# A transformer kernel on one core: the squares of a residual are summed on VectorE before TensorE takes them, and a stage's first two product blocks are interleaved by row

## The reference

```python
def rms_norm(x, gain):
    xf = x.astype(jnp.float32)
    y = xf * lax.rsqrt(jnp.mean(xf * xf, axis=-1, keepdims=True) + EPS)
    return (y * gain.astype(jnp.float32)).astype(x.dtype)
...
h = h + mix                                    # residual, r = 1, 5, 10, 14
h = h + conv_ffn(rms_norm(h, ffn_norm[layer]), ...)   # residual, r = 4, 8, 13, 17
```

## Time and profile before

| | |
|---|---|
| runs, us | 2889.69, 2891.96, 2896.49 |
| profiled execution, its own time | 2890.2 us |
| its span | 2888.4 us |
| mean granted TensorE clock | 0.985 of 2.4 GHz |
| busy: TensorE, VectorE, ScalarE, GpSimd | 96%, 60%, 36%, 3% |

### The profile page before, as it was taken

The page is one execution under the profiler, slowest core; times in us unless marked ns, Lnnn a source line. Parts: engine busy times, 40 slices in busy tenths (PEclk is TensorE's granted clock), DMA queues, the critical chain, the costliest instruction groups (busy, mean ns, idle before and its releaser), DMA issues.

```text
span 2888.4 us, 35842 instructions
## 1 busy us (share of the span) xinstructions
PE 2773.1 (96%) x14656; PEld 2250.6 (78%) x14656; DVE 1728.3 (60%) x2488; ACT 1028.3 (36%) x1495; POOL 90.1 (3%) x156
## 2 busy tenths in 40 slices
PE   7999799999998999999999999999999999999998
PEld 6778688888875588888776688888888787888886
DVE  4287657475668557575556647564665888553443
ACT  3244434242333534242434633232332222432322
POOL 0000000000001300000001400000000000000000
PEclk9999999999999999999999999999999999999999
DMA  6711024443232124343321025454432110333221
GB/s 162 158 44 44 30 89 149 126 143 108 73 97 81 30 85 153 124 141 111 88 82 44 1 65 193 159 178 138 143 100 70 34 33 26 107 104 100 88 92 41
DMA packets 261803, 276.85 MB, mean 96 GB/s; under 512 B 23496, under 2 KB 230856, under 8 KB 261641
## 3 DMA queue, kind: packets, MB, share of 16 engines
q1 hardware_dynamic: 231448, 219.51, 25.0%
q10 hardware_dynamic: 30192, 55.05, 5.9%
HBM read 267.19 MB, written 7.34 MB: 95 GB/s over the span
## 4 chain that ended last, share of the span: by engine, by line
PE 86%; DVE 7%; ACT 2%; DMA 2%; issue 1%; SPq 1%; ACTq 0%; POOL 0%; DVEq 0%
PE ps L554 23%; PE ps L556 23%; PE ps L555 23%; PE ps L1154 3%; PE ps L790 2%; PE ps L1186 2%; PE ps L918 1%; DMA sb<-in_hgrn_w_in 1%; PE ps L1113 1%; PE ps L935 1%; PE ps L612 1%; DVE sb L1826 1%; PE ps L1132 1%; DVE sb L2192 1%; PE ps L952 1%
## 5 line engine op out<-in xcount | busy, mean ns | idle before, releaser
L554 PE MATMUL ps<-sb 128*128 128x512 f32 (+2 forms) x3448 | 1286.7, 373 | 31.6 <-ACT sb L1388 5.5
L556 PE MATMUL ps<-sb 128*128 128x512 f32 (+2 forms) x3448 | 1268.0, 368 | 0.0
L555 PE MATMUL ps<-sb 128*128 128x512 f32 (+2 forms) x3448 | 1267.9, 368 | 0.0
L554 PEld LDWEIGHTS ps<-sb 128*128 128x128 f32 x3448 | 651.2, 189 | 162.0 <-issue 36.0
L556 PEld LDWEIGHTS ps<-sb 128*128 128x128 f32 x3448 | 650.7, 189 | 112.4
L555 PEld LDWEIGHTS ps<-sb 128*128 128x128 f32 x3448 | 651.3, 189 | 108.9 <-issue 1.2
L1826 DVE TENSOR_TENSOR sb<-sb 128x2048 fp32r<-128x2048 f32 (+2 forms) x196 | 438.4, 2237 | 357.8 <-ACT sb L1287 357.8
L1287 ACT ACTIVATE sb<-sb 128x2048 fp32r<-128x2048 f32 (+2 forms) x196 | 365.0, 1862 | 286.1 <-PE ps L556 266.7
L2062 DVE SCALAR_TENSOR_TENSOR sb<-ps,sb 128x511 f32<-128x511 f32 (+1 forms) x264 | 197.5, 748 | 172.2 <-ACT sb L1511 166.7
L1511 ACT ACTIVATE sb<-ps,sb 128x512 f32<-128x512 f32 x132 | 99.7, 772 | 233.7 <-PE ps L556 233.6
L2082 DVE SCALAR_TENSOR_TENSOR sb<-sb 128x512 f32<-128x512 f32 x168 | 126.0, 750 | 12.9 <-DVE sb L2082 0.5
(11 more groups left out here) (226 smaller groups left out, 2170.8 us busy)
## 6 DMA issues: line engine op xcount, KB each, us to landing
sb<-in_ffn_w_up SPq DMA_DIRECT2D x88, 1024.0 KB, 5.1
sb<-in_ada_w ACTq DMA_DIRECT2D x192, 256.0 KB, 3.2
sb<-in_ffn_w_down SPq DMA_DIRECT2D x32, 1024.0 KB, 5.0
sb<-in_ffn_w_down SPq DMA_DIRECT2D x16, 768.0 KB, 4.4
sb<-in_hy_w_in SPq DMA_DIRECT2D x12, 1024.0 KB, 5.1
sb<-in_hgrn_w_in SPq DMA_DIRECT2D x8, 1024.0 KB, 11.5
sb<-in_hgrn_w_in SPq DMA_DIRECT2D x16, 512.0 KB, 5.5
sb<-in_dsa_w_in SPq DMA_DIRECT2D x6, 1024.0 KB, 5.2
```

Source lines behind the costliest of these rows:

```text
L554: pe.matmul(o, al, bh, start=f, stop=False, **kw)
L555: pe.matmul(o, ah, bl, start=False, stop=False, **kw)
L556: m = pe.matmul(o, ah, bh, start=False, stop=l, **kw)
```

## The change

Two things change. First, VectorE adds up the squares of tiles 0 to 5: the square of tile 0 is written to `total` (`sq[1]`), the squares of tiles 1 to 6 to `one` (`sq[0]`), and `accumulate` adds `one` to `total` after tiles 1 to 5. TensorE sums `total` once, after the last block's first part, then tiles 6 and 7. The addition for tile j-1 stands on VectorE behind the addition of x tile j; the one for tile 5 behind `ahead(keys[2])`. The square of tile j waits for the addition of tile j-1, the square of tile 7 for TensorE's sum of `total`. At r = 8 both sets are treated so. Second, `halved_start` takes both blocks together for the first half: per row 12 matmuls, for 4 banks, which are waited for at the start; the second half's last sums stand after row 2, its spreading after row 5.

```diff
--- before.py
+++ after.py
@@ -650,8 +650,7 @@
                     project_half(key, j, 0, b, range(kt), ready, tile).then_inc(*mark(sem, ("res", r, 6 + j, 0)))
                     freed[b] = [("x", r, 6 + j, 0)]
                     if j == 0:
-                        squared(4)
-                        squared(5)
+                        squared(None)
                 for j in range(2):
                     b, part = banks[0][j], (kt - 2, kt // 2)[j]
                     wait_bank(b)
@@ -667,30 +666,35 @@
             def halved_start(sem, r, keys, banks, done, then):
 
                 stage, i = NEXT[r]
-                for half in range(2):
-                    ready = lambda k: [("h", stage, half, k, "hi"), ("h", stage, half, k, "lo")]
+                ready = lambda half, k: [("h", stage, half, k, "hi"), ("h", stage, half, k, "lo")]
+                for n in range(2):
+                    for b in banks[n]:
+                        wait_bank(b)
+                for k in range(NT):
                     for n in range(2):
-                        if half == 0:
-                            for b in banks[n]:
-                                wait_bank(b)
-                        for k in range(NT):
-                            for j in range(2):
-                                m = project_half(keys[n], j, half, banks[n][j], (k,), ready)
-                                if half and k == NT - 1:
-                                    m.then_inc(*mark(sem, done[n][j], *([("used", keys[n])] if j else [])))
-                                    freed[banks[n][j]] = then[n][j]
-                            if half == 0 and n == 0 and k == 2:
-                                squared_half(r, 1)
-                        if half == 0 and n == 0:
-                            spread_half(stage, i, 1)
-
+                        for j in range(2):
+                            project_half(keys[n], j, 0, banks[n][j], (k,), lambda k: ready(0, k))
+                    if k == 2:
+                        squared_half(r, 1)
+                    elif k == 5:
+                        spread_half(stage, i, 1)
+                for n in range(2):
+                    for k in range(NT):
+                        for j in range(2):
+                            m = project_half(keys[n], j, 1, banks[n][j], (k,), lambda k: ready(1, k))
+                            if k == NT - 1:
+                                m.then_inc(*mark(sem, done[n][j], *([("used", keys[n])] if j else [])))
+                                freed[banks[n][j]] = then[n][j]
             def residual(sem, r, keys, banks, ready, tile=None, stats=True, gain=False, amid=None, late=None):
                 def squared(j):
+
                     for i in ((0, 1) if gain else (0,)):
-                        if j == 0:
+                        if j is None:
                             wait_bank((STAT, OTHER)[i])
-                        pe.wait_ge(*at("sq", r, i, j))
-                        sums((STAT, OTHER)[i], (ht if i else sq)[j % 2], j == 0, j == NT - 1).then_inc(
+                            pe.wait_ge(*at("acc", r, i, 5))
+                        else:
+                            pe.wait_ge(*at("sq", r, i, j))
+                        sums((STAT, OTHER)[i], (ht if i else sq)[1 if j in (None, 7) else 0], j is None, j == NT - 1).then_inc(
                             *mark("pe_stat", ("sq_used", r, i, j), *([("stat", r, i)] if j == NT - 1 else [])))
 
                 for n in range(4):
@@ -706,14 +710,10 @@
                         halved_end(sem, r, keys[n], banks, ready, tile, squared)
                     elif stats and n == 3:
                         project(sem, keys[n], banks[n % 2], names, then, tile=tile, ready=ready, cols=(0,))
-                        squared(4)
-                        squared(5)
+                        squared(None)
                         project(sem, keys[n], banks[n % 2], names, then, tile=tile, ready=ready, cols=(1,))
                     else:
                         project(sem, keys[n], banks[n % 2], names, then, tile=tile, ready=ready)
-                        if stats and n:
-                            squared(2 * n - 2)
-                            squared(2 * n - 1)
                 if stats and r not in NEXT:
                     squared(6)
                     squared(7)
@@ -1337,7 +1337,7 @@
             def squares_half(r, j, half):
                 hs = HALVES[half]
                 act.wait_ge(*at("x", r, j, half))
-                act.wait_ge(*at("sq_used", r, 0, j - 2))
+                act.wait_ge(*(at("acc", r, 0, 5) if j == 6 else at("sq_used", r, 0, None)))
                 act.activation(sq[j % 2][:, hs], x[:, j, hs], ACTF.Square).then_inc(*mark("act_sq", ("sq", r, 0, j, half)))
 
             def squares(r, j, gain):
@@ -1346,9 +1346,11 @@
                 for i in ((0, 1) if gain else (0,)):
                     g = v("final_norm", j) if i else 1.0
                     act.wait_ge(*at("x", r, j))
-                    dst = (ht if i else sq)[j % 2]
-                    if j >= 2:
-                        act.wait_ge(*at("sq_used", r, i, j - 2))
+                    dst = (ht if i else sq)[1 if j in (0, 7) else 0]
+                    if j == 7:
+                        act.wait_ge(*at("sq_used", r, i, None))
+                    elif j >= 2:
+                        act.wait_ge(*at("acc", r, i, j - 1))
                     act.activation(dst[:, :], x[:, j, :], ACTF.Square, scale=g).then_inc(*mark("act_sq", ("sq", r, i, j)))
 
             def residual(r, keys, stats=True, gain=False):
@@ -1920,7 +1922,16 @@
                 dve.wait_ge(*at("g1", stage, 1))
                 normalise_halves(r, lambda j: g1c[:, j:j + 1], base, then)
 
-            def residual(r, banks, keys, scale=None, stats=True):
+            def accumulate(r, j, gain):
+
+                for i in ((0, 1) if gain else (0,)):
+                    one, total = ht if i else sq
+                    dve.wait_ge(*at("sq", r, i, j))
+                    if j > 1:
+                        dve.wait_ge(*at("acc", r, i, j - 1))
+                    dve.tensor_tensor(total[:, :], total[:, :], one[:, :], ADD).then_inc(*mark("dve_acc", ("acc", r, i, j)))
+
+            def residual(r, banks, keys, scale=None, stats=True, gain=False):
                 ended[r] = banks, scale
                 for n in range(4):
                     if r in NEXT and n == 3:
@@ -1936,8 +1947,12 @@
                         else:
                             m = dve.scalar_tensor_tensor(x[:, j, :], ps[b][:, :], mod[:, scale + j:scale + j + 1], x[:, j, :], MUL, ADD)
                         m.then_inc(*mark("dve_x", ("x", r, j)))
+                        if stats and 2 <= j < 6:
+                            accumulate(r, j - 1, gain)
                     if n < 3 or not stats:
                         ahead(keys[n])
+                    if stats and n == 2:
+                        accumulate(r, 5, gain)
 
             def begin():
                 for i in range(2):
@@ -2114,7 +2129,7 @@
                             ada(slot)
                             slot += 1
                 gi = len(GROUPS) - 1
-                residual(r0 + gi, ((0, 1), (4, 5)), [(stage, "down", gi, j) for j in range(4)], scale)
+                residual(r0 + gi, ((0, 1), (4, 5)), [(stage, "down", gi, j) for j in range(4)], scale, gain=n == 1)
                 if n in ADA:
                     layer, b0, blocks = ADA[n]
                     c0, width = 4 * b0, 4 * blocks
```

## The result

The changed kernel takes 2927.76 us (median of 4 runs, 2922.59 to 2929.84) beside 2893.07 for the kernel before: a ratio of 1.0117, 95% interval 1.0099 to 1.0136, or +34 us (34.7 between the medians). The prediction said slower, 2909, at most 2919. The direction and the stall came as written; the size is twice the forecast, outside its range, since two of its four terms were wrong. The profiled execution is the fastest of the four: 2922.59 us, span 2920.8, 32.4 more than before. Three views give nearly all of it.

A forecast was written before the change was run, and what follows sets the result against it. TensorE, busy 2773.1 of 2888.4 us, was taken as the bound. Terms -12.5 + 31.5 - 9.3 + 8 = +17.7 on the profiled 2890.2 gave 2907.9, about 2909 us for the median; the 8-in-10 range was 2892 to 2919.

The forecast's parts named there:

- the stall: At residual ends except r = 17, TensorE stands still for VectorE's sum with tile 5, 4.1 to 4.7 us each.
- What bounds the kernel, and where: Whole kernel: TensorE busy 2773.1 of 2888.4 us, so nearly all change to its stream or waits is time; eight residual ends.
- Sums removed, -12.5 us: Residual ends: TensorE's sums fall from three groups to one; -10.0 us at seven ends, -2.5 at r = 8.
- Sums added, +31.5 us: Residual ends: TensorE waits for VectorE's addition of tile 5, behind the low split; +31.5 us, bounds 24 and 36.
- E+7.6: At r = 1, the sum with tile 5 is done 7.6 us after TensorE finishes the third block (E).
- The order of the first blocks, -9.3 us: Stage starts: 12 matmuls per row end starvation, less a bank wait; gain 1.4 or 1.7 us at six stages, -9.3.
- The clock, +8 us: After new TensorE idle stretches: clock falls to half at two of three of seven ends, 1.7 us each; bounds 0, +14.
- The clock holds: Rival, the seven ends: no clock loss, everything else as forecast, without the +8 us; 2901.7 us, chance 0.17.
- The reorder gives all: Rival, stage starts: bank wait small or absorbed, -17 for -9.3, and no clock loss; +2 us, 2894, chance 0.12.
- The lower clock lasts: Rival, the seven ends: 2.5 us lost to the clock at each; +27 us, 2919, chance 0.03.
- Faster: the last sum is covered: Rival, residual ends: TensorE does not stand still at the sum with tile 5; -21.8 us, 2870, chance 0.12.
- its deciding point: Residual ends: with TensorE standing still less than 3.1 us per end, the change is not slower.

The follow-up runs named there:

- the filler: Changed kernel with 18 extra matmuls, their result overwritten, in each of TensorE's seven waits for the sum with tile 5; 2908.75 us beside 2890.34, ratio 1.0062.
- the lagging second block: Against sums on VectorE, tile 5 before split, later total, early-form new order: second block one row behind, its banks awaited only then; 2864.3 us, ratio 0.9906.
- the kernel before that edit: Against the kernel before: sums on VectorE, tile 5 before split, total after tile 7's first half, new order with earlier statistic; 2873.75 us, ratio 0.9933.

## Why the prediction was wrong, step by step

*What bounds the kernel, and where.* Right. The part with the sums makes the loss alone (+34 us by itself), and a TensorE wait was worth its length.

*Sums removed, -12.5 us.* Right: the instructions of L612 fell from 704 to 344, as worked out. With the sum moved ahead of the split the part gives -8 us with 4.5 us of waits left (six, 0.9 at most), and -13 without them.

*Sums added, +31.5 us.* Right: 32.3 us in the list of waits, 4.83 at r = 1 against 4.6, and none at the last residual for the split. The chain came within 0.2 us: last sum at 390.41 with the third block ended at 382.7, E+7.7 for a predicted E+7.6. That its place behind the split is the cause is shown: moved one place up, 32.3 us of waits become 4.5.

*The order of the first blocks, -9.3 us.* This step failed; the part alone measured +1 us (-3 to +4). The wait for the bank was seen (1.18 us at r = 1, foreseen 1.3; 9.2 in all) and the starvation ended. What failed is, first, the size of the gain: 5.1 us at the end of the first half's products and not 9.3. At r = 1 it is 1.0 for 1.4; at r = 13 the bank's wait was 2.05 us, and the lower clock behind it, for which the sum had no term, took the gain. Second, and of the same weight, the gain was followed only as far as the rows of the second half. I had worked out that they come 1.5 us later (1.9 in the trace) and checked them only against the products of those rows, where they do hold. I did not follow VectorE on to its next work, the split and the first convolutions, which free the banks of the second gate block. Counted from the first half's spreading at r = 1 (397.79 before, 401.40 after), the convolutions end at 28.1 us before and TensorE comes at 28.7, 0.6 behind them; in the changed kernel they end at 28.6 and TensorE is there at 27.9. It became a wait at four FFNs, 4.9 us.

*The clock, +8 us.* The mechanism was right and its size was half. I took two of three ends and 3.4 us of low clock at each; it fell at all seven and lasted 3.1 to 6.0 us of work, 14.8 us lost by the distances, 16 by the filler. The rule of the Trainium skill (TensorE: Matmul & The Clock Gate, Part 1), that a pause between bursts of matmuls sends the clock back to its lower level, applied to all seven ends was nearer than my share of two thirds. At these ends the traces agree with it, 7 of 7 at 0.50.

Together, -12.5 + 32.3 + 14.8 + about 1 is 35.6 for a measured 34: of the excess over the forecast's 18 the clock makes 7, the order 10 and the stall 1, with 2 us the other way. The profiled execution of after was the fastest of four; its 32.4 us and the median's 34 differ by less than those runs do. That the direction was right is no luck, since it rests on the stall, which came as foreseen.

*The rivals.* "The clock holds" fell by the seven stretches at 0.50 and by the filler. "The reorder gives all" fell by the new order alone, +1 us. "The lower clock lasts" took 2.5 us lost per end, of which 2.1 came, and was still 9 us too low, since it kept the 9.3 us of the order. "Faster: the last sum is covered" is not what the change does, but its deciding point was right: with 0.6 to 0.9 us per end in place of 4.6 the kernel is faster than before.

Open: why this trace has fewer or more falls of the clock in the HGRN stage (up to five short ones between 105 and 310 us in some executions, none in others). They make a few us between executions of one kernel and were not studied.

## What to carry to other kernels

A new instruction costs what stands before it in its engine's program, not its own 0.69 us: look for the longest instruction ahead of it, and put what TensorE waits for in front of what nobody needs yet. Price a pause of TensorE of some microseconds with the slow stretch behind it, here nearly half as much again (14.8 us for 32.3). And when a step makes TensorE earlier and its supplier later, follow the supplier to its next deadline, not only through the rows at hand; a wait for all buffers at the start is best put off to each buffer's first use.

## Not expected of the hardware

Pauses of about 2 us were followed by the lower clock too: in the kernel with the filler TensorE waits 2.05 us for the bank at 2110.11, and then

```profile
2110.20:2112.00 1.80, 0.00 (x0) 0.00 (x0) 1.70 (x5) 0.27 (x2) 0.00 (x0) 0.88 0.00 0
2112.20:2114.90 2.70, 2.70 (x13) 2.70 (x14) 2.00 (x6) 1.40 (x4) 0.00 (x0) 0.50 0.00 0
```

while in the earlier trace rows one of 2.6 us was not. All seven traces that have this wait of 2.05 us at r = 13 show the fall; of the waits of 1.8 us at r = 4, in the same traces, four of seven are followed by one.

It is a part of what the lagging second block gained. First the kernel before that edit, the bank's wait and the products behind it at r = 13 and the products at r = 4, then the lagging one at the same places:

```profile
2082.20:2084.10 1.90, 0.00 (x0) 0.00 (x0) 1.80 (x5) 0.37 (x2) 0.00 (x0) 1.00 0.00 0
2084.30:2087.60 3.30, 3.30 (x16) 3.30 (x17) 2.24 (x5) 1.32 (x4) 0.00 (x0) 0.50 0.00 0
...
777.10:780.30 3.20, 3.20 (x16) 3.03 (x15) 1.41 (x4) 0.42 (x1) 0.00 (x0) 0.50 0.00 0
...
2080.50:2090.00 9.50, 9.47 (x81) 8.77 (x80) 8.15 (x19) 4.58 (x11) 0.00 (x0) 1.00 0.01 2
768.00:790.00 22.00, 20.79 (x172) 19.15 (x172) 16.99 (x41) 9.98 (x24) 0.00 (x0) 1.00 0.12 29
```

Both falls are gone. Half of 6.5 us, at most 3.2 us, came from there (an estimate from these rows), beside the 9.2 us of waits; 0.9 us of new waits for rows go the other way. How the 9.5 us divide exactly was not separated.
